# Weight blocks of a two-block transformer stack stored in interleaved pairs and read with a step of two elements

## The reference

```
q, k, v, u, g = jnp.split(h_lat @ w_in, splits, axis=-1)     # first stack, layer 0
q, k, v, g = jnp.split(h_lat @ w_in, splits, axis=-1)        # first stack, layer 1
a = dwconv3(h @ w_in, conv_w, conv_b); return (jax.nn.silu(gate) * up) @ w_out
q, k, v, o, gi, gf, xb, gate = _split(hn @ w_in, AB_SPLITS)  # second stack, layer 0
a = jax.nn.relu(hn @ w1); return (a * a) @ w2
```

## Time and profile before

| | |
|---|---|
| Median of 3 runs | 2000.32 us (1997.08 to 2002.23) |
| Profiled execution, its own time | 2003.57 us |
| Its span | 2001.8 us |
| Mean granted TensorE clock | 0.987 |
| PE busy, weight loads (PEld) busy | 95%, 85% of the span |
| DVE, ACT, POOL busy | 62%, 46%, 11% |
| PE's share of the chain that ended last | 83% |
| DMA | 296.79 MB, mean 148 GB/s |

### The profile page before, as it was taken

One profiled execution on the slowest core, in us unless ns is written; L12 is line 12 of the kernel. 1 busy time (PEld: TensorE's weight loads), 2 busy tenths in 40 slices (PEclk: granted clock), 3 DMA queues, 4 the chain that ended last, 5 costly groups with the idle time before them and its releaser, 6 DMA issues.

```text
span 2001.8 us, 33468 instructions
## 1 busy us (share of the span) xinstructions
PE 1907.4 (95%) x13373; PEld 1697.0 (85%) x13373; DVE 1239.6 (62%) x1853; ACT 920.6 (46%) x1441; POOL 229.6 (11%) x179
## 2 busy tenths in 40 slices
PE   5999979999999899999899998999999999989998
PEld 3776657778888589999889997998899999879997
DVE  6355355543664546677577768656875567787564
ACT  5344343322332422177475554357553445665453
POOL 2100104430552000022000000000010010000001
PEclk9999989999999999999999999999999999989999
DMA  9611465433222433222445553532345554224553
GB/s 389 239 61 64 168 232 185 166 115 113 91 85 93 183 125 107 89 101 85 168 153 177 198 177 128 176 134 91 127 169 181 177 172 145 95 95 169 192 187 127
DMA packets 43952, 296.79 MB, mean 148 GB/s; under 512 B 4976, under 2 KB 6129, under 8 KB 11697
## 3 DMA queue, kind: packets, MB, share of 16 engines
q1 hardware_dynamic: 36576, 247.48, 35.6%
q10 hardware_dynamic: 6048, 42.50, 5.9%
q0 software_dynamic: 1200, 5.02, 0.7%
HBM read 293.94 MB, written 1.05 MB: 147 GB/s over the span
## 4 chain that ended last, share of the span: by engine, by line
PE 83%; DVE 10%; ACT 4%; issue 2%; DMA 1%; POOL 1%; ACTq 0%; DVEq 0%; POOLq 0%
PE acc L462 23%; PE acc L463 23%; PE acc L464 22%; DVE w_lo L397 2%; PE acc L457 2%; PE acc L459 2%; PE acc L458 2%; PE wk L555 1%; PE wk L1733 1%; ACT w_hi L387 1%; PE acc L1722 1%; PE wk L1462 1%; DVE X L1073 1%; DVE nt L1079 1%; PE acc L1483 1%
## 5 line engine op out<-in xcount | busy, mean ns | idle before, releaser
L397 DVE TENSOR_TENSOR w_lo<-w_raw,w_hi 128x1024 fp32r<-128x1024 f32 (+2 forms) x472 | 574.3, 1255 | 177.2 <-ACT w_hi L387 175.6
L462 PE MATMUL acc<-Hhi,w_hi 128*128 128x272 f32 (+2 forms) x2048 | 654.1, 319 | 20.6 <-DVE Hlo L826 7.6
L387 ACT ACTIVATE w_hi<-w_raw 128x1024 fp32r<-128x1024 f32 (+2 forms) x472 | 452.4, 1005 | 424.3 <-PE acc L464 332.9
L463 PE MATMUL acc<-Hlo,w_hi 128*128 128x272 f32 (+2 forms) x2048 | 637.2, 311 | 0.0
L464 PE MATMUL acc<-Hhi,w_lo 128*128 128x272 f32 (+2 forms) x2048 | 635.8, 310 | 0.0
L462 PEld LDWEIGHTS acc<-Hhi,w_hi 128*128 128x128 f32 x2048 | 389.6, 190 | 67.8 <-issue 39.3
L464 PEld LDWEIGHTS acc<-Hhi,w_lo 128*128 128x128 f32 x2048 | 388.2, 190 | 19.5
L463 PEld LDWEIGHTS acc<-Hlo,w_hi 128*128 128x128 f32 x2048 | 389.1, 190 | 18.1
L462 PE MATMUL acc<-Fhi,w_hi 128*128 128x256 f32 (+2 forms) x864 | 262.6, 304 | 3.2 <-POOL Flo L1152 1.5
L464 PE MATMUL acc<-Fhi,w_lo 128*128 128x256 f32 (+2 forms) x864 | 261.9, 303 | 0.0
L463 PE MATMUL acc<-Flo,w_hi 128*128 128x256 f32 (+2 forms) x864 | 261.9, 303 | 0.0
(11 more groups left out here) (415 smaller groups left out, 2667.0 us busy)
## 6 DMA issues: line engine op xcount, KB each, us to landing
w_raw<-in_w_ffn_in SPq DMA_DIRECT2D x44, 1024.0 KB, 4.8
ada_ring<-in_w_ada ACTq DMA_DIRECT2D x40, 1024.0 KB, 5.8
w_raw<-in_w_mlp_in SPq DMA_DIRECT2D x32, 1024.0 KB, 4.8
w_raw<-in_w_mlp_out SPq DMA_DIRECT2D x32, 1024.0 KB, 4.8
w_raw<-in_w_ffn_out SPq DMA_DIRECT2D x32, 704.0 KB, 4.0
ada_first<-in_w_ada SPq DMA_DIRECT2D x8, 1024.0 KB, 20.4
w_raw<-in_w_ret_v SPq DMA_DIRECT2D x8, 1024.0 KB, 5.0
w_raw<-in_w_ret_g SPq DMA_DIRECT2D x8, 1024.0 KB, 4.7
```

The lines of the kernel that those rows point to most:

```text
L387: act.activation(w_hi[:, r, a:b], w_raw[:, r, a:b], ACT.Copy).then_inc(hi_done, 1)
L397: dve.tensor_tensor(w_lo[:, r, a:b], w_raw[:, r, a:b], w_hi[:, r, a:b].bitcast(F32), ALU.subtract).then_inc(lo_done, 1)
L462: pe.matmul(o, w_hi[:, r, w], x_hi(k), start=k == 0, stop=False)
L463: pe.matmul(o, w_hi[:, r, w], x_lo(k), start=False, stop=False)
```

## The change

On the host, each slot of every projection that is not token-major is stored so that blocks 2i and 2i+1 are interleaved element by element: in each partition, element `2m` of a pair is column `m` of the even block and element `2m + 1` is column `m` of the odd one. A last block without a partner (11 blocks) stays as it was. DMA, `w_raw`, ACT's copy and DVE's subtraction go over the same number of floats in the same order of addresses and are not changed. In `project` the stationary operand is read with a step of two elements, 128 floats out of 1024 bytes, instead of 128 neighbours out of 512 bytes. The instructions of all engines, their order and their waits are the same as before.

```diff
+        def stationary(w, r, p, j):
+
+            if j == p.K * p.C - 1 and j % 2 == 0:
+                return w[:, r, j * P:(j + 1) * P]
+            return w[:, r, j // 2 * 2 * P + j % 2:(j // 2 + 1) * 2 * P:2]
...
                     else:
-                        w = slice((k * p.C + c) * P, (k * p.C + c + 1) * P)
-                        pe.matmul(o, w_hi[:, r, w], x_hi(k), start=k == 0, stop=False)
-                        pe.matmul(o, w_hi[:, r, w], x_lo(k), start=False, stop=False)
-                        mm = pe.matmul(o, w_lo[:, r, w], x_hi(k), start=False, stop=k == last)
+                        b_hi, b_lo = stationary(w_hi, r, p, k * p.C + c), stationary(w_lo, r, p, k * p.C + c)
+                        pe.matmul(o, b_hi, x_hi(k), start=k == 0, stop=False)
+                        pe.matmul(o, b_hi, x_lo(k), start=False, stop=False)
+                        mm = pe.matmul(o, b_lo, x_hi(k), start=False, stop=k == last)
...
+def _paired(w, blocks):
+
+    n = w.shape[0]
+    pairs = w[:, :, :blocks // 2 * 2 * P].reshape(n, P, blocks // 2, 2, P).transpose(0, 1, 2, 4, 3)
+    return np.concatenate([pairs.reshape(n, P, -1), w[:, :, blocks // 2 * 2 * P:]], 2)
...
+    for p in PROJ:
+        if p.kind != "tok":
+            arrays["w_" + p.name] = _paired(arrays["w_" + p.name], p.K * p.C)
```

## The result

The changed kernel takes 2034.13 us (2031.47 to 2036.83, 4 runs) against 2001.28 us before (the median of 4 runs now). The ratio is 1.0175 with a 95% interval of 1.0156 to 1.0194; run again later on another occasion it was 1.0169 (1.0143 to 1.0195). So the change costs 33 to 35 us. The forecast was 1970 us, a gain.

The account below looks back on a forecast made before the run. PE's matmul pitch was taken as the bound. Savings of 13.5 and 2.2 us (272 columns), 9.3 and 2.9 (256) and 2.5 (512) made 30 us, from the 2000.3 us median to 1970 us; likeliest case 1960 to 1985, range 1940 to 2050.

Parts of the forecast that it names:

- What bounds the kernel: Whole kernel: PE, busy for 95% of the span, so the pitch of 10,320 matmuls; ACT, DVE and DMA cost nothing.
- point 1 of the change, part by part: What it could remove: pitch above the common rate at 256, 272 and 512 columns, all on PE, at most about 30 us.
- The lock: Load and moving streams sharing one rate stay free of collisions; forecast case of −15 to −40 us, chance 0.47.
- the free state at 113.3 ns: 256-column matmuls at 18 pitches in 2.04 us, read as a load and moving stream locked without collisions; 1296 matmuls already there.
- The common rate: 0.443 ns per column, from 226.7 / 512 and 113.3 / 256; by it 272 columns would need 120.4 ns.
- twice the interference: Rival: the load touches twice the bytes and meets the moving stream twice as often; +45 us, 2045 us, chance 0.24.
- the load as the bound: Rival: a load with a step lasts over 125 ns and sets the pitch at 256 and 272 columns; 2795 us, chance 0.06.
- The upper bound of gain: All above bare streaming vanishes, with loads at 110 ns from four 128-column turns; together 73 us of gain, 1927 us.
- The upper bound of loss: A step of two halves the load's pace to 220 ns, hidden at 512 columns, paid at 256 and 272; 795 us.
- the rival of no effect: The two streams don't touch each other's reads; the 113 and 118 ns states come from something else; 2000 us, chance 0.15.

## Why the prediction was wrong

**What bounds the kernel:** right. PE's pitch was the whole question, the loss adds up over matmuls, and ACT, DVE and DMA could be costed at nothing: their groups kept their means, and PE's wait at the line is 20.8 us against 20.6.

**The step that failed** is point 1 of the change, part by part: "If the load still lasts as long, both streams advance at nearly one rate, and a relation that is free of collisions once stays free." Its condition is false: the load's own pace went from 111.5 to 118.2 ns, and at 256 columns, where load and matmul are equally long, that nearly is the pitch (120.0). And no free relation survived: the stages at 113.3 ns went to 120.0 as well, and 30 us of gain became 36 us of pitch. The lock was put in place of a price that I had no row for, and the row I called nearest, the free state at 113.3 ns, said only that contiguous loads can be free of disturbance.

**The common rate** of 0.443 ns per column, from which the 120.4 ns at 272 columns and with it half of the gain was worked out, was read off two points. A third, 384 columns, has 173.4 ns and not 170; the excess over bare streaming (0.417 ns a column, the estimate from these widths) is 13.3 ns at 320, 384 and 512 columns alike and 6.7 at 256. It is no rate.

**The bounds.** The rival on the other side, twice the interference, gave 2045 us and had 0.24; the time was 2034. Its prices of 4.6 ns were 6.6 at 512 columns, up to 6.7 at 256 and 2.2 at 272, and its reason was half right: the disturbance of a moving stream by a load that it covers exists at 480 and 512 columns, but is 1.6 ns or less from 288 to 448, and it doesn't go with how much the load reads (229.9 ns with half a load, 226.7 with a whole one, contiguous). The largest share of the loss, 16.2 of 36.3 us at 256 columns, belongs to the rival that I held least likely, the load as the bound, with a price of 7 ns instead of 100. I had noted that load and matmul are "already within 3 ns of each other (110 and 113.3)" and took it as an argument for a remote case; it was the plainest fact of the profile: with two things equally long, anything that lengthens either is paid in full, while a gain in the other is not. That should have carried the forecast: a change that at best leaves the load as it is can't bring any stage below the load's 111.5 ns, and had 2 to 6 ns to win at 256 columns, while whatever it adds to the load lifts the floor under every 256-column stage.

**The upper bound of gain**, 110 ns from four turns of 128 columns, was about right as the load's pace (111.5 over 314 matmuls).

**The upper bound of loss**, a load at half its pace with 795 us, stayed away at a step of two, where the load takes 118.2 ns, and came with a step of four (235.5 ns). I had no row that told the two apart. The 512-column stages, 226.7 against 233.3 ns with a load of 118, speak against the rival of no effect, by which the two streams don't touch each other's reads; what it is that holds the matmul up there isn't shown.

**Open** is why a covered load of pairs costs 6.6 ns at 512 columns, 3.3 at 480, 2.0 to 3.4 at 272 and nothing at 320, 384 and 448, so the mechanism behind 20 of the 36 us; and what puts a 256-column stage with contiguous weights at 113.3, 116.7 or 117.8 ns. A price on the moving stream by the amount that the load reads, and the rows' distance in the first stack, were tried and ruled out; no theory of mine fits all the widths.

## What to carry to other kernels

Before a change to how an operand is read, compare the pitch of the matmuls with the pace of the load alone (a run with a short moving operand shows it): here 113 to 118 ns against 111.5 before, so at 256 columns there was little to gain on the matmul side, and a longer load was paid. Keep float32 weights and above all float32 moving operands contiguous: here a step of two cost the load 6% (111.5 to 118.2 ns) and a moving operand 100% (113.4 to 229.9), and a step of four doubled the load too (235.5). And a rate drawn through two widths is a guess; one more width tells a share from a fixed charge.

## What was unexpected of the hardware

- The pitch isn't a rate plus a constant: above 0.417 ns a column (the estimate from 320, 384 and 512 columns) the excess is 6.7, 10 or 11 ns at 256 columns, about 12 at 272 (125.2), 13.3 at 320 and 384, 17 at 448 (203.5), 16.7 at 480 and 13.3 at 512, and is steady over hundreds of matmuls.
- The same stage can run at 113.3 or 117.8 ns for nearly its whole length; ret_out changed from one to the other between two kernels that don't differ there. With pairs this choice vanished.
- Loads with steps of 2, 3 and 4 took 0.456 to 0.462 ns per float of the stretch that they lie over, and a moving operand of 256 columns 0.443 to 0.449, contiguous or with a step of two (an estimate from the readings above).
- At half the clock (0.50 granted) a load takes 213 ns whether contiguous or in pairs, while with a step of four the pitch is 235 ns at either clock, with 128 columns at 0.50 and with 256 at 1.00.
- Cutting the stationary operand to 64 columns didn't shorten the pitch at 512 columns (229.9 ns against 226.7): it became longer. At 256 columns 64 stationary columns took 119.0 ns contiguous and 115.6 with a step of two.
